# A hybrid decoder layer on one core: the first norm's weights travel with x, and x and the first weight block arrive in three pieces

## The reference, cut to what matters

```python
def rmsnorm(t, gain):
    tf = t.astype(F32)
    out = tf * lax.rsqrt(jnp.mean(tf * tf, axis=-1, keepdims=True) + NORM_EPS) * gain.astype(F32)
    return out.astype(t.dtype)

def hybrid_layer(h, mem, cos, sin, mix_norm_gain, w_in, gate_bias, ...):
    n = rmsnorm(h, mix_norm_gain)
    proj = n @ w_in
    att_p, rwkv_p, memq_p, gate_p = split_last(proj, (ATT_IN, RWKV_IN, MEM_W, GATE_IN))
...
    h = h + merged @ w_out
    h = h + peer_ffn(rmsnorm(h, ffn_norm_gain), peer_w_q, peer_key1, peer_key2, peer_u, peer_v)
    return h
```

## Time and profile before

| what | us |
|---|---|
| median of 3 runs | 1049.82 (1049.78 to 1057.03) |
| span of the profiled execution, first to last instruction | 1047.7 |
| what the median has beyond that span | 2.1 |
| PE busy | 831.4 (79% of the span) |
| DVE busy | 644.8 (62%) |
| ACT busy | 390.1 (37%) |
| POOL busy | 343.9 (33%) |

### The profile page before, as it was taken

How to read it: one execution, slowest core, us unless ns; L and a number is a source line. 1 busy time by engine, 2 the same in 40 slices (tenths; PEclk the granted TensorE clock), 3 DMA queues, 4 the chain that set the end, 5 groups by cost and what they waited for, 6 DMA issues and landing times.

```text
span 1047.7 us, 16371 instructions
## 1 busy us (share of the span) xinstructions
PE 831.4 (79%) x5744; PEld 488.2 (47%) x5744; DVE 644.8 (62%) x1570; ACT 390.1 (37%) x1102; POOL 343.9 (33%) x307
## 2 busy tenths in 40 slices
PE   9999999999999999766875875766666656656655
PEld 8887888788888887422422422321111111111111
DVE  4543550487343428886686686686685785785784
ACT  2025142215220102744443543444443443443443
POOL 1000000510020004445355355355445445455441
PEclk9999999999999999988888888778767667667667
DMA  8443423222223297999999999999999999999996
GB/s 347 146 149 126 160 104 134 81 82 87 78 93 111 102 415 276 425 427 427 426 427 426 426 428 426 426 426 426 426 426 428 426 428 427 427 428 427 428 426 282
DMA packets 46874, 329.66 MB, mean 315 GB/s; under 512 B 5344, under 2 KB 5600, under 8 KB 7520
## 3 DMA queue, kind: packets, MB, share of 16 engines
q0 software_dynamic: 36864, 268.45, 60.8%
q1 hardware_dynamic: 9104, 57.65, 15.2%
q10 hardware_dynamic: 848, 2.75, 0.7%
HBM read 327.78 MB, written 1.05 MB: 314 GB/s over the span
## 4 chain that ended last, share of the span: by engine, by line
PE 50%; DMA 27%; DVE 12%; issue 5%; ACT 4%; POOL 1%; POOLq 0%; DVEq 0%; ACTq 0%; SPq 0%
DMA pool_mem<-in_experts,pool_mem 27%; PE psum_proj L639 11%; PE psum_job L1100 7%; PE psum_proj L1012 7%; DVE pool_mem L2009 5%; PE psum_proj L1075 5%; PE psum_proj L1038 4%; PE psum_proj L652 3%; PE psum_job L880 2%; DVE pool_mem L1899 1%; PE psum_job L1059 1%; PE psum_proj L1059 1%; ACT pool_mem L1425 1%; DVE pool_mem L1896 1%; ACT pool_mem L1422 1%
## 5 line engine op out<-in xcount | busy, mean ns | idle before, releaser
L1100 PE MATMUL psum_job<-pool_mem 64*64 64x512 f32 x2048 | 350.9, 793 | 204.3 <-ACT pool_mem L1425 196.3
L2108 POOL DMA_INDIRECT pool_mem<-in_experts,pool_mem x256 | 309.0, 1207 | 393.4 <-PE psum_job L1100 264.0
L2009 DVE CUSTOM_DVE_ANT_0 pool_mem<-pool_mem 128x1024 f32<-128x1024 f32 x256 | 309.6, 1224 | 163.9 <-DMA pool_mem<-in_experts,pool_mem 162.7
L1100 PEld LDWEIGHTS psum_job<-pool_mem 64*64 64x64 f32 x2048 | 83.1, 162 | 452.3 <-issue 451.2
L1418 ACT ACTIVATE pool_mem<-pool_mem 128x1 f32<-128x1 f32 x256 | 51.6, 201 | 262.7 <-DVE pool_mem L2009 256.8
L639 PE MATMUL psum_proj<-pool_mem 128*128 128x256 f32 x544 | 118.9, 379 | 0.0
L639 PEld LDWEIGHTS psum_proj<-pool_mem 128*128 128x128 f32 x544 | 103.0, 190 | 15.1 <-issue 1.3
L1425 ACT ACTIVATE pool_mem<-const,pool_mem 128x64 f32<-128x64 f32 x256 | 89.1, 348 | 18.4
L1422 ACT ACTIVATE pool_mem<-pool_mem 128x1 f32<-128x1 f32 x256 | 75.4, 294 | 9.3
L1012 PE MATMUL psum_proj<-pool_mem 128*128 128x256 f32 x320 | 74.0, 384 | 0.0
L1075 PE MATMUL psum_proj<-pool_mem 128*128 128x256 f32 (+1 forms) x320 | 65.4, 360 | 4.7 <-ACT pool_mem L1454 2.5
(11 more groups left out here) (293 smaller groups left out, 858.1 us busy)
## 6 DMA issues: line engine op xcount, KB each, us to landing
pool_mem<-in_weights SPq DMA_DIRECT2D x50, 1024.0 KB, 4.9
pool_mem<-in_experts,pool_mem POOLq DMA_INDIRECT x256
pool_mem<-in_weights ACTq DMA_DIRECT2D x2, 512.0 KB, 6.4
pool_mem<-in_xT SPq DMA_DIRECT2D x2, 512.0 KB, 6.3
pool_mem<-in_memT SPq DMA_DIRECT2D x1, 1024.0 KB, 10.9
pool_mem<-in_x ACTq DMA_DIRECT2D x1, 1024.0 KB, 12.3
const<-in_const SPq DMA_DIRECT2D x1, 825.5 KB, 14.2
rows<-in_rows SPq DMA_DIRECT2D x1, 512.0 KB, 16.1
```

What stands on the lines that cost most here:

```text
L1100: ins = mm(sum_bank(t, d)[sum_strip(i, d), :], lhsT=diag[rows_, g % DIAGS, :], rhs=slot[g % SLOTS][rows_, D + 512 * d:D + 512 * d + 512], ...
L2009: ins = V.tensor_tensor_reduce(u, u, xn_tok[:, t, :], 1.0, 0.0, ALU.mult, ALU.add, hid[:, par, s_:s_ + 1])
L2108: G_.indirect_dma_start(slot[s_ % SLOTS], None, t_in["experts"], bass.IndirectOffsetOnAxis(ap=expert_i[:, par, s_:s_ + 1], axis=0)).then_i ...
```

## The change

It does five things.

1. The 8 columns of `mix_norm_gain` leave `vec` (now 78 columns) and stand in front of x in the array `xT`, which is now 2056 columns wide. In SBUF they lie in the 8 columns in front of `in_sq["x"]`, so that one DMA fills both.
2. x comes in three pieces of 256, 256 and 512 KB (the first with the 4 KB of gains): slabs 0 and 1, slabs 2 and 3, slabs 4 to 7.
3. Block 0 comes in the same three pieces.
4. `vec` is issued after block 1, and DVE waits for it only ahead of the mixing loop.
5. PE multiplies ones by ones 8 times, not 13.

```diff
-for _name, _n in [("mix_gain", 8), ("mem_gain", 8), ("gate_bias", 24), ...
+for _name, _n in [("mem_gain", 8), ("gate_bias", 24), ...
...
+        gained_x = part(Q0 - KT, KT + KT * S)
+        mix_gain = part(Q0 - KT, KT)
...
-            for j in range(2):
-                sp.dma_start(in_sq["x"][:, 4 * j:4 * j + 4, :].rearrange("p a b -> p (a b)"),
-                             t_in["xT"][:, 1024 * j:1024 * j + 1024]).then_inc(x_in[j], 16)
-                if j == 0:
-                    sp.dma_start(vec[:, :], t_in["vec"]).then_inc(vec_in, 16)
+            for j, (a, b) in enumerate(((0, KT + 2 * S), (KT + 2 * S, KT + 4 * S), (KT + 4 * S, KT + KT * S))):
+                sp.dma_start(gained_x[:, a:b], t_in["xT"][:, a:b]).then_inc(x_in[j], 16)
             for b in range(1, RING):
                 sp.dma_start(wring[b].rearrange("p a b -> p (a b)"), t_in["weights"][b]).then_inc(weights_in[b], 16)
                 if b == 1:
+                    sp.dma_start(vec[:, :], t_in["vec"]).then_inc(vec_in, 16)
                     sp.dma_start(mT.rearrange("p a b -> p (a b)"), t_in["memT"]).then_inc(mem_in, 16)
...
-            for _ in range(13):
+            for _ in range(8):
                 mm(psum_job[:, BANKS - 1, 0:P], lhsT=ones[:, :], rhs=ones[:, :], start=True, stop=True)
             o = begin_bank(unit("rwkv", 0))
             for j in range(4):
-                pe.wait_ge(first_in if j < 2 else weights_in[0], 16)
+                pe.wait_ge(first_in[j] if j < 2 else weights_in[0], 16)
...
-                for j in range(2):
-                    act.dma_start(wring[0][:, 4 * j:4 * j + 4, :].rearrange("p a b -> p (a b)"),
-                                  t_in["weights"][0][:, 1024 * j:1024 * j + 1024]).then_inc(weights_in[0] if j else first_in, 16)
+                for arrived, a, b in ((first_in[0], 0, 2), (first_in[1], 2, 4), (weights_in[0], 4, KT)):
+                    act.dma_start(wring[0][:, a:b, :].rearrange("p a b -> p (a b)"),
+                                  t_in["weights"][0][:, 256 * a:256 * b]).then_inc(arrived, 16)
...
-            dve.wait_ge(vec_in, 16)
             for j in range(4):
 
-                dve.wait_ge(x_in[j // 2], 16)
+                dve.wait_ge(x_in[min(j, 2)], 16)
                 for k in (2 * j, 2 * j + 1):
-                    ins = V.tensor_scalar(nT[:, k, :], in_sq["x"][:, k, :], v("mix_gain", k), None, ALU.mult)
+                    ins = V.tensor_scalar(nT[:, k, :], in_sq["x"][:, k, :], mix_gain[:, k:k + 1], None, ALU.mult)
                 ins.then_inc(sg["x_gained"], 1)
...
             dve.wait_ge(sg["mix_pad"], 1)
+            dve.wait_ge(vec_in, 16)
...
-        "x": a["x"][0], "xT": _channel_major(a["x"][0]), ...
+        "x": a["x"][0], "xT": np.concatenate([_vec(a["mix_norm_gain"]), _channel_major(a["x"][0])], axis=1), ...
```

More of the change, by code:

```diff
@@ L87 @@
 _c = 0
-for _name, _n in [("mix_gain", 8), ("mem_gain", 8), ("gate_bias", 24), ("mu", 14), ("w0", 4), ("a0", 4),
+for _name, _n in [("mem_gain", 8), ("gate_bias", 24), ("mu", 14), ("w0", 4), ("a0", 4),
                   ("k_k", 4), ("k_a", 4), ("r_k", 4), ("q_gain", 1), ("k_gain", 1), ("mq_gain", 1), ("mk_gain", 1), ("ffn_gain", 8)]:
@@ L417, in build @@
         mem_in = sem("mem_in")
-        x_in = [sem(f"x_in{j}") for j in range(2)]
-        first_in = sem("first_in")
+        x_in = [sem(f"x_in{j}") for j in range(3)]
+        first_in = [sem(f"first_in{j}") for j in range(2)]
         late_in = sem("late_in")
@@ L2154 @@
     vec = np.concatenate([
-        _vec(a["mix_norm_gain"]), _vec(a["mem_norm_gain"]), _vec(a["gate_bias"][0][list(BRANCH_ORDER)]), _vec(a["rwkv_mu"]),
+        _vec(a["mem_norm_gain"]), _vec(a["gate_bias"][0][list(BRANCH_ORDER)]), _vec(a["rwkv_mu"]),
         _vec(a["rwkv_w0"]), _vec(a["rwkv_a0"]), _vec(a["rwkv_k_k"]), _vec(a["rwkv_k_a"]), _vec(a["rwkv_r_k"]),
@@ L2158 @@
     arrays = {
-        "x": a["x"][0], "xT": _channel_major(a["x"][0]), "memT": _channel_major(a["mem"][0]), "positions": a["positions"].reshape(S), "const": constants(), "vec": vec,
+        "x": a["x"][0], "xT": np.concatenate([_vec(a["mix_norm_gain"]), _channel_major(a["x"][0])], axis=1), "memT": _channel_major(a["mem"][0]), "positions": a["positions"].reshape(S), "const": constants(), "vec": vec,
         "lora": np.concatenate([a["rwkv_w2"][0], a["rwkv_a2"][0]]), "glora": a["rwkv_g2"][0],
```

## The result

The changed kernel takes 1062.5 us (median of 6 runs, 1061.8 to 1063.3) against 1050.4 us for the kernel before on the same chip. The ratio is 1.0107, with a 95% interval of 1.0089 to 1.0125. The forecast was 1048.8 with a range of 1048.2 to 1051.0: the change was to be worth a microsecond and costs twelve.

The account below looks back on a forecast made before the run. The prediction saw PE busy without a gap, then gathers at the DMA limit. A gain of 1.1 us at the product for the squares, less 0.1 for the clock, took 1049.8 to 1048.8 us; range 1048.2 to 1051.0.

Parts of the forecast that it names:

- rival C: Start or PEER stage: the gain is lost to a later last piece of x or slower PEER stage; 1049.8 us, chance 0.15.
- A's worst case: Unit 0 on PE: run wholly at the lower clock level, it ends at 19.7 us, 5.3 us slower, 1055 us.
- The start of unit 0: PE's first useful product: starts at T = 5.9 us, not 7.34, once first pieces of x and block 0 land.
- The last piece of x: Middle of unit 0: the last 512 KB of x lands at 8.85 us, about 0.1 us earlier than before.
- the gain of 1.1: PE's product for the squares: begins at 13.2 us, not 14.33, so 1.1 us earlier.
- The fold and the sum of squares: DVE's fold ends 0.1 us earlier, at 13.1 us; PE's product for the squares follows at 13.2.
- Unit 2 and its bank: After unit 1 on PE: unit 2 needs unit 0's bank, emptied by DVE from 19.45 to 20.14 us, which doesn't move.
- this cap: Unit 2 on PE: waiting for unit 0's bank limits the gain at the start to about 1.4 us.
- The clock: Unit 0 on PE: fewer products of ones may leave its first passes at the lower clock; 0.1 to 0.2 us lost.
- rival A: Unit 0 on PE: the clock rises too late after fewer ones and a pause; 1050.6 to 1055 us, chance 0.3.
- rival B: Start: the quarters land no earlier than the halves did; gain only 0.4 us, 1049.4 us, chance 0.15.
- The carry-over: From the start to the kernel's end: a microsecond won at the start moves everything behind it, 1.0 us in all.

Follow-up runs that it names:

- first run: The changed kernel with only the vector's SBUF tensor as wide as before, so the gather slots lie at their old addresses: 1051.7 us.
- second run: The kernel before with the vector's SBUF tensor 8 columns wider, shifting everything behind it by 32 bytes: 1062.8 us, ratio 1.0104.
- eleventh run: The kernel before with only x and block 0 in pieces of 256, 256 and 512 KB: 1051.0 us, ratio 0.9996.
- sixteenth: The kernel before with 8 unused columns in front of x's array in HBM (pitch 8224 bytes): 1055.6 us, ratio 1.0045.
- eighth: The changed kernel with slots at their old addresses, x and block 0 in halves of 512 KB, 8 products of ones: 1054.7 us.
- ninth run: The changed kernel with slots at their old addresses, x and block 0 in halves of 512 KB, 13 products of ones: 1053.6 us.

## Why the prediction was wrong

**What failed is the premise that carries the start's gain to the end: "a microsecond won at the start moves everything behind it", with, in rival C, "gathers that run at the limit whenever they begin".** They do run with full engines, but at what rate depends on where the slots lie (427 or 419 GB/s here), and the change moved them. The prediction went through everything that the diff adds, removes and reorders, and never asked what else moves when a tensor shrinks. The sum puts the gathers' own length at no change, without a term for it; the term is +11.6 us in the two profiles (10.8 us between the medians of the changed kernel and the first run, on another chip, and 11.2 us between the second run and the kernel before). The chance of 0.01 for a loss of over 1% rested on "Slower by over 1% needs twice A's worst case", that is on the belief that only the first 20 us could change.

**The start of unit 0** (T = 5.9, between 5.3 and 6.9): measured 6.16. Right, with some luck: 5.9 was chosen between two bounds, one of them counted in bytes at 333 to 369 GB/s, and the stretch ran at 229.

**The last piece of x** (8.85 us): measured 10.44, 1.6 us late. This is the second step that failed, and it took away the gain of 1.1: the sum of squares stands at 14.73 and not at 13.2. The step took the bytes ahead of the piece as its price, at the rate that the trace before shows for other packets from another layout. Both edits cost rate: pieces alone bring the last one at 10.10 (eleventh run), the layout alone at 9.85 (sixteenth). The slower rate with pieces alone (2.21 MB in the first 9 us for 2.58) agrees in its direction with the rule of the Trainium skill that the prediction weighed and set aside ("DMA: Bandwidth & Descriptors", section "Rules for kernel authors"); it accounts for one of the two.

**The fold and the sum of squares** (0.1 us earlier): they followed the last piece as the step says, only the other way: 8.95 to 10.44 on DVE, 13.20 to 14.67 for the fold's end, 14.73 on PE.

**Unit 2 and its bank**: PE went on without a wait, though DVE began to empty the bank later as well (at 21.34 for 19.45, behind `memT`). So "that doesn't move" was wrong. By the prediction's own reckoning unit 2 would have asked for the bank near 20.6, with the sum of squares at 13.2, and here the bank came free only at 22.03 (21.34 + 0.69). With these loads this cap alone would have taken the forecast gain.

**The clock** (0.1 to 0.2 us): in the profiled run the first eight passes took 1.96 us, the upper level, after 3.46 us of ones and a pause of 1.69. So rival A did not happen there. Its mechanism is real all the same: in three runs with pauses of 2.4 to 3.5 us unit 0 took 9.33, 8.78 and 10.03 us for 7.14, and in the last of them the sum of squares came at 19.63, where the prediction's worst case had 19.7. More products of ones are at best a partial protection: the eighth and ninth run (8 and 13) differ by 2.0 us, but the runs with 8.78 and 10.03 us had 13 products. With one profile each this is not shown beyond doubt.

**Rival C** had the late last piece, and its sign ("after 9.5") was there, but it put the price at no more than the gain; **rival B** didn't happen.

**The carry-over** was right: the second L667 of the trace stands at 28.57 us before and at 29.16 after, and the first gather is issued the same 0.6 us later (400.8 and 401.4).

## What to carry to other kernels

When an edit changes the size of any on-chip tensor, compare the addresses of everything declared behind it before looking at the edit itself, and above all those of DMA destinations: keep them at multiples of 256 bytes, since in this stage, bound by DMA, 32 bytes too few cost 1.9% of its rate. A load that is pulled out of one array and glued to another changes that array's pitch, and small pieces that land early can make the last piece land late; what decides is the last one. Where PE has to pause ahead of its first products, look at how long they take: after pauses of 2.4 us and more some of them ran at half the clock here. And before a tenth of a microsecond at the start is believed, compare profiles whose start is the same: here they differed by 0.5 us.

## What the runs showed of the hardware that was not expected

- Gathers of 8 KB rows into slots at 32, 64 or 128 bytes past a multiple of 256, or 32 short of one, run at 419 to 421 GB/s, at a multiple at 426 to 427.
- Right at the start of the program, from 3 to 6 us, the core's DMA engines moved 341 to 359 GB/s when x lay in HBM in rows with a pitch of 8192 bytes, and 258 to 269 with 8224 or 284 with 8448; with x and block 0 in pieces, from plain rows, 312. In the first 9 us that was 2.57 to 2.62 MB with plain rows in halves, and 2.18 to 2.24 MB with either edit alone.
- When TensorE's clock rises differs from run to run of nearly the same start: 26 passes of ones from 1.01 us on took between 4.57 and 5.91 us in these profiles (26 at the lower level take 5.9), and after pauses of 2.5 and 2.7 us unit 0 ran at the upper level, after 2.4 in another run partly at the lower.
